# Stick-breaking attention: key blocks from last to first in three groups, and the order of the heads' steps on each engine

## The reference, cut to what matters

```python
q = rmsnorm(qkv[:, :, 0], q_norm)      # k likewise, v as it is
for blk in range(S // 128):            # queries q0 .. kend
    z = einsum("bhtd,bhsd->bhts", q[:, :, q0:kend], k[:, :, :kend]) * scale
    strict = key < query
    log_1mb = where(strict, log_sigmoid(-z), 0.0)
    between = cumsum(log_1mb, axis=3, reverse=True) - log_1mb
    att = where(strict, exp(log_sigmoid(z) + between), 0.0)
    out = einsum("bhts,bhsd->bhtd", att, v[:, :, :kend])
```

## Time and profile before

| | busy us | share of the span |
|---|---|---|
| TensorE (PE) | 3024.0 | 98% |
| VectorE (DVE) | 2709.6 | 87% |
| GpSimd (POOL) | 1680.2 | 54% |
| ScalarE (ACT) | 1495.0 | 48% |

### The profile page before, as it was taken

The page is one execution under the profiler, slowest core; times in us unless marked ns, Lnnn a source line. Parts: engine busy times, 40 slices in busy tenths (PEclk is TensorE's granted clock), DMA queues, the critical chain, the costliest instruction groups (busy, mean ns, idle before and its releaser), DMA issues.

```text
span 3098.5 us, 45070 instructions
## 1 busy us (share of the span) xinstructions
PE 3024.0 (98%) x15648; PEld 2701.9 (87%) x15648; DVE 2709.6 (87%) x4904; ACT 1495.0 (48%) x2668; POOL 1680.2 (54%) x989
## 2 busy tenths in 40 slices
PE   7999999999999999999999899999999999999999
PEld 6888899999999888888777678999999998888887
DVE  7987997999999889998687769989999999888887
ACT  4344335766665333343444643346666663333332
POOL 3434356888896555542245433467988986422221
PEclk9999999999999999999899899999999999999999
DMA  6633246999999999999335342357999999999996
GB/s 258 241 103 123 82 150 214 317 336 356 323 343 368 382 386 393 382 392 375 111 110 175 84 134 82 106 183 259 362 334 337 346 342 378 381 373 368 350 350 234
DMA packets 320605, 846.16 MB, mean 273 GB/s; under 512 B 28208, under 2 KB 149056, under 8 KB 320400
## 3 DMA queue, kind: packets, MB, share of 16 engines
q1 hardware_dynamic: 189952, 437.83, 41.0%
q0 software_dynamic: 74000, 268.81, 23.6%
q10 hardware_dynamic: 56448, 136.86, 11.7%
HBM read 735.91 MB, written 94.90 MB: 268 GB/s over the span
## 4 chain that ended last, share of the span: by engine, by line
PE 80%; DVE 11%; ACT 3%; issue 2%; POOL 2%; DMA 2%; SPq 0%; ACTq 0%; DVEq 0%; POOLq 0%
PE banks L1179 22%; PE gbank L1179 11%; PE banks L1159 9%; PE banks L1161 9%; PE banks L1160 9%; PE banks L1139 4%; PE banks L1141 4%; PE banks L1140 4%; DVE u_rows L2151 3%; PE gbank L1531 2%; POOL w_lo L593 1%; DVE hot L2128 1%; PE gbank L1485 1%; PE banks L1251 1%; POOL u_rows L610 1%
## 5 line engine op out<-in xcount | busy, mean ns | idle before, releaser
L593 POOL TENSOR_TENSOR w_lo<-raw,w_hi 128x1024 fp32r<-128x1024 f32 x351 | 868.7, 2476 | 567.6 <-ACT w_hi L685 563.7
L685 ACT ACTIVATE w_hi<-raw 128x1024 fp32r<-128x1024 f32 x613 | 646.8, 1055 | 603.6 <-PE banks L1179 350.5
L618 POOL DMA_INDIRECT v_rows<-v_dram,row_of x256 | 376.6, 1471 | 598.6 <-DVE fetched L2166 585.1
L1159 PE MATMUL banks<-h_hi,w_hi 128*128 128x384 f32 x2048 | 686.6, 335 | 2.7 <-POOL w_lo L593 2.7
L1160 PE MATMUL banks<-h_lo,w_hi 128*128 128x384 f32 x2048 | 684.7, 334 | 0.0
L1161 PE MATMUL banks<-h_hi,w_lo 128*128 128x384 f32 x2048 | 684.5, 334 | 0.0
L2151 DVE CUSTOM_DVE_ANT_0 u_rows<-u_rows,h_rows 128x1024 f32<-128x1024 f32 x256 | 449.8, 1765 | 5.3 <-DMA u_rows<-u_dram,row_of 5.2
L610 POOL DMA_INDIRECT u_rows<-u_dram,row_of x256 | 359.7, 1405 | 135.3 <-DVE z L2151 97.0
L1159 PEld LDWEIGHTS banks<-h_hi,w_hi 128*128 128x128 f32 x2048 | 384.7, 188 | 4.4 <-POOL w_lo L593 4.4
L1160 PEld LDWEIGHTS banks<-h_lo,w_hi 128*128 128x128 f32 x2048 | 384.5, 188 | 0.0
L1161 PEld LDWEIGHTS banks<-h_hi,w_lo 128*128 128x128 f32 x2048 | 384.4, 188 | 0.0
(11 more groups left out here) (377 smaller groups left out, 5079.2 us busy)
## 6 DMA issues: line engine op xcount, KB each, us to landing
raw<-stream_dram SPq DMA_DIRECT2D x613, 512.0 KB, 6.3
gel_dram<-gel ACTq DMA_DIRECT2D x248, 192.0 KB, 5.0
gin<-gel_dram SPq DMA_DIRECT2D x62, 768.0 KB, 10.5
g_dram<-stage ACTq DMA_DIRECT2D x56, 768.0 KB, 11.0
gates<-g_dram SPq DMA_DIRECT2D x64, 672.0 KB, 7.4
ada_w<-ada_dram ACTq DMA_DIRECT2D x34, 512.0 KB, 6.3
ada_out<-ada_dram ACTq DMA_DIRECT2D x18, 512.0 KB, 4.8
ada_first<-ada_dram SPq DMA_DIRECT2D x8, 1024.0 KB, 17.6
```

Of the source, the lines that this page charges most:

```text
L593: pool.tensor_tensor(w_lo[:, s, :], raw[:, s, :], w_hi[:, s, :].bitcast(F32), ALU.subtract).then_inc(split_lo, 1)
L618: pool.indirect_dma_start(v_rows[:, j % V_ROWS, :], None, (v0, v1)[layer], bass.IndirectOffsetOnAxis(ap=row_of[:, j:j + 1], axis=0)).then_ ...
L685: act.activation(w_hi[:, s, :], raw[:, s, :], ACT.Copy).then_inc(split_hi, 1)
L1159: pe.matmul(out, wh, h_hi[:, k, 0:DENSE_T], start=(k == 0), stop=False)
```

## The change

Three things change. First, the key blocks are kept and worked in the order 3, 2, 1, 0, in three groups: blocks 3 and 2 together (384 columns), block 1 (384), block 0 (512). ScalarE, VectorE and GpSimd do one instruction a group in place of one a block; the mask of blocks 3 and 2 is one product. Second, each wait of the products, of the casts and of the weights counts groups: the products of keys n start when the high part of their group is there, and `sp_hi` of h+1 may be rewritten group by group. Third, the order of the heads' steps is another on every engine: TensorE does the products of h, the logits of h+2, the weighted sum of h; ScalarE the Exp and Ln of h, the weights of h-1, the output copy of h-2; VectorE the sign passes of h, the output's low part of h-3, the max passes and low parts of h. GpSimd splits one side (q or k) after each head, where it split both after every second. Three constant tiles move to the place of a tile of layer 0. `att` stays one buffer.

```diff
@@ -166,7 +166,7 @@
 LOW_ROW = 32
 
 
-KEY_AT = [sum(SEQ - n * P for n in range(j)) for j in range(CH)]
+KEY_AT = [sum(SEQ - n * P for n in range(j + 1, CH)) for j in range(CH)]
 KEPT_KEYS = sum(SEQ - n * P for n in range(CH))
 STACKED = 6 * 16
 STACK_FROM = 21
@@ -175,6 +175,11 @@
 def from_key(j):
 
     return slice(KEY_AT[j], KEY_AT[j] + SEQ - j * P)
+
+
+GROUPS = 3
+GROUP_OF = (2, 1, 0, 0)
+GROUP_KEYS = (slice(0, from_key(2).stop), from_key(1), from_key(0))
 
 OUT_DOTS, V_DOTS, QKV_DOTS = 6, 18, 12
 V_COL = OUT_DOTS
...
@@ -437,13 +442,17 @@
 
 
         b = (bank, misc)[h % 2][min(j, 2)]
-        return b[:, 0:P] if j == 3 else b[:, n * P:]
+        return b[:, P:2 * P] if j == 3 else b[:, n * P:]
+
+    def zgroup(h, g):
+
+        b = (bank, misc)[h % 2][2 - g]
+        return b[:] if g == 2 else b[:, P:]
 
     def obank(h):
 
         return (bank, misc)[h % 2][3]
 
-    together = (1, 2, 4, 4)
 
     block = ctx.enter_context(nc.Block())
 
...
@@ -641,17 +650,21 @@
 
         lows(RING, DENSE0 + U_EARLY + LOW_AHEAD)
         peer(0)
-        def split_heads(m):
+        def split_side(m, n):
 
             pool.wait_ge(S("qk_done"), DC + m + 1)
             for half in range(2):
                 wait(pool, S(f"stacked{half}"), STACKED * (m - 1))
-            for n, x in enumerate((aq, ak)):
-                pool.tensor_copy(qk_hi[:, m % 2, n, :], x[:, m, :]).then_inc(S("qk_hi"), 1)
-            for n, (lo, x) in enumerate(((q_lo, aq), (k_lo, ak))):
-                pool.wait_ge(S("qk_hi"), 2 * m + n + 1)
-                pool.tensor_tensor(lo[:, m, :], x[:, m, :], qk_hi[:, m % 2, n, :].bitcast(F32), ALU.subtract
-                                   ).then_inc(S("qk_lo"), 1)
+            x, lo = ((aq, q_lo), (ak, k_lo))[n]
+            pool.tensor_copy(qk_hi[:, m % 2, n, :], x[:, m, :]).then_inc(S("qk_hi"), 1)
+            pool.wait_ge(S("qk_hi"), 2 * m + n + 1)
+            pool.tensor_tensor(lo[:, m, :], x[:, m, :], qk_hi[:, m % 2, n, :].bitcast(F32), ALU.subtract
+                               ).then_inc(S("qk_lo"), 1)
+
+        def split_heads(m):
+
+            for n in range(2):
+                split_side(m, n)
 
         lows(DENSE0 + 2 * NKEYS, QKV1 + 13)
         split_heads(0)
@@ -660,15 +673,15 @@
         lows(QKV1 + 17, OUT1 + LEAD)
         def stick_highs(h):
 
-            wait(pool, S("logw"), CH * h)
-            for j in range(CH):
-                pool.wait_ge(S("sp"), CH * h + j + 1)
-                pool.tensor_copy(sp_hi[:, from_key(j)], sp[:, h % 2, from_key(j)]).then_inc(S("sp_hi"), 1)
+            for g, own in enumerate(GROUP_KEYS):
+                wait(pool, S("logw"), GROUPS * (h - 1) + g + 1 if h else 0)
+                pool.wait_ge(S("sp"), GROUPS * h + g + 1)
+                pool.tensor_copy(sp_hi[:, own], sp[:, h % 2, own]).then_inc(S("sp_hi"), 1)
 
         for h in range(SB_HEADS):
             stick_highs(h)
-            if h % 2 == 0 and h // 2 + 2 < DC:
-                split_heads(h // 2 + 2)
+            if h // 2 + 2 < DC:
+                split_side(h // 2 + 2, h % 2)
         lows(OUT1 + LEAD, DENSE1 + U_EARLY + LOW_AHEAD)
         peer(1)
 
@@ -1086,18 +1099,19 @@
 
         def sticks(h):
 
-            for j in range(CH):
-                act.wait_ge(S("z_abs"), CH * h + j + 1)
-                zs = sp[:, h % 2, from_key(j)]
+            for g, own in enumerate(GROUP_KEYS):
+                act.wait_ge(S("z_abs"), GROUPS * h + g + 1)
+                zs = sp[:, h % 2, own]
                 act.activation(zs, zs, ACT.Exp, scale=-1.0).then_inc(S("z_exp"), 1)
-                act.wait_ge(S("z_exp"), CH * h + j + 1)
+                act.wait_ge(S("z_exp"), GROUPS * h + g + 1)
                 act.activation(zs, zs, ACT.Ln, bias=1.0).then_inc(S("z_ln"), 1)
 
         def weights(h):
-            for j in range(CH):
-                act.wait_ge(S("logw"), CH * h + together[j])
-                wait(act, S("att_out"), h)
-                act.activation(att[:, from_key(j)], zq(h, j, j), ACT.Exp).then_inc(S("att"), 1)
+
+            wait(act, S("att_out"), h)
+            for g, own in enumerate(GROUP_KEYS):
+                act.wait_ge(S("logw"), GROUPS * h + g + 1)
+                act.activation(att[:, own], zgroup(h, g), ACT.Exp).then_inc(S("att"), 1)
 
         def mixed(h):
             o = HD * (h % 2)
@@ -1105,13 +1119,14 @@
             act.activation(h_hi[o:o + HD, h // 2, :], obank(h)[o:o + HD, :], ACT.Copy
                            ).then_inc(S("o_hi"), 1)
 
-        sticks(0)
         for h in range(SB_HEADS):
-            if h + 1 < SB_HEADS:
-                sticks(h + 1)
-            if h:
-                mixed(h - 1)
-            weights(h)
+            sticks(h)
+            if h >= 1:
+                weights(h - 1)
+            if h >= 2:
+                mixed(h - 2)
+        weights(SB_HEADS - 1)
+        mixed(SB_HEADS - 2)
         mixed(SB_HEADS - 1)
         projected_out(1)
         peer(1)
@@ -1587,50 +1602,56 @@
 
             q, k_hi, k_lo_ = (stacks[h % 2][:, n, :] for n in range(3))
             pe.wait_ge(S(f"stacked{h % 2}"), STACKED * (h // 2 + 1))
-            for j in range(CH):
-                if 2 <= h and j < 3:
-                    pe.wait_ge(S("att"), CH * (h - 2) + together[j])
+            for j in (3, 2, 1, 0):
+                if h >= 2 and j != 2:
+                    pe.wait_ge(S("att"), GROUPS * (h - 2) + GROUP_OF[j] + 1)
                 for k in (k_hi, k_lo_):
-                    pe.matmul(zq(h, j, j), k[:, j * P:(j + 1) * P], q[:, j * P:], start=(j < 3 and k is k_hi),
+                    pe.matmul(zq(h, j, j), k[:, j * P:(j + 1) * P], q[:, j * P:], start=(j != 2 and k is k_hi),
                               stop=False, skip_group_check=True)
-                last = pe.matmul(zq(h, j, j)[:, 0:P], identb[:], masked[:], start=False, stop=True,
-                                 skip_group_check=True)
-                if j != 2:
-                    last.then_inc(S("z"), 2 if j == 3 else 1)
+                if j == 2:
+                    both = [P, 2, P]
+                    diag = zgroup(h, 0)[:, 0:2 * P].rearrange("p (j t) -> p j t", j=2)
+                    pe.matmul(diag, identb[:], masked[:].unsqueeze(1).to_broadcast(both), start=False, stop=True,
+                              skip_group_check=True).then_inc(S("z"), 1)
+                elif j < 2:
+                    pe.matmul(zq(h, j, j)[:, 0:P], identb[:], masked[:], start=False, stop=True,
+                              skip_group_check=True).then_inc(S("z"), 1)
 
         def log_weights(h):
 
-            pe.wait_ge(S("sp_hi"), CH * (h + 1))
-            pe.wait_ge(S("sp_lo"), CH * (h + 1))
-            for j in range(CH):
+            pe.wait_ge(S("sp"), GROUPS * (h + 1))
+            for n in (3, 2, 1, 0):
+                if n != 2:
+                    pe.wait_ge(S("sp_hi"), GROUPS * h + GROUP_OF[n] + 1)
                 for part_ in (sp_hi, sp_lo):
-                    last = pe.matmul(zq(h, j, j), negtri_r[:], part_[:, from_key(j)], start=False, stop=True,
+                    if n != 2 and part_ is sp_lo:
+                        pe.wait_ge(S("sp_lo"), GROUPS * h + GROUP_OF[n] + 1)
+                    last = pe.matmul(zq(h, n, n), negtri_r[:], part_[:, from_key(n)], start=False, stop=True,
                                      skip_group_check=True)
-                    for n in range(j + 1, CH):
+                    for j in range(n):
                         last = pe.matmul(zq(h, j, n), negones_r[:], part_[:, from_key(n)], start=False,
                                          stop=True, skip_group_check=True)
-                if j != 2:
-                    last.then_inc(S("logw"), 2 if j == 3 else 1)
+                if n != 3:
+                    last.then_inc(S("logw"), 1)
 
         def weighted(h):
             both = slice(P * (h // 2), P * (h // 2) + P)
             if h >= 2:
                 pe.wait_ge(S("o_hi"), h - 1)
                 pe.wait_ge(S("o_lo"), h - 1)
+            pe.wait_ge(S("att"), GROUPS * (h + 1))
             for j in range(CH):
-                pe.wait_ge(S("att"), CH * h + j + 1)
                 last = pe.matmul(obank(h)[:, j * P:], av[:, j, both], att[:, from_key(j)],
                                  start=(j == 0), stop=(j == CH - 1), skip_group_check=True)
             last.then_inc(S("att_out"), 1)
 
-        logits(0)
+        for h in range(2):
+            logits(h)
         for h in range(SB_HEADS):
-            if h + 1 < SB_HEADS:
-                logits(h + 1)
-            if h:
-                weighted(h - 1)
             log_weights(h)
-        weighted(SB_HEADS - 1)
+            if h + 2 < SB_HEADS:
+                logits(h + 2)
+            weighted(h)
         pe.wait_ge(S("o_lo"), SB_HEADS)
         for m in range(N_OUT - 2):
             h_tile(OUT1 + m)
@@ -2274,24 +2295,27 @@
         link(biased(2 * DC, OUT1_COL))
```

(51 more changed lines are left out.)

## The result

The changed kernel took 3077.56 us (median of 4 runs, 3076.86 to 3081.25) against 3099.84 for the kernel before (median of 4): the ratio is 0.9932, with a 95% interval of 0.9915 to 0.9949, so 22.3 us less where 21.0 were forecast. The profiled execution took 3076.86 us, 23.4 less than the profiled one before.

What follows compares the result with a forecast made beforehand. Layer 1's attention was taken as bound by a ring of waits between engines, no engine full. Fifteen heads of 7.1 us plus a 15.9 us last frame end it at 1799.8, 21.0 less: 3100.3 to 3079.3, range 3071 to 3092.

Steps and rivals of the forecast that it cites:

- The ring, and what opens it: Layer 1's attention: no engine full; removing TensorE's 2.31 us gap before logits keeps the clock up, saving 1.66 us a pair.
- VectorE's frame: One head's passes on VectorE in layer 1's attention: period 7.15 us for twelve heads, 6.85 for three, mean 7.1.
- TensorE: TensorE's work in one head: 6.6 us at the higher clock, under the period, with 0.5 us of slack.
- Merging: Three groups instead of four instructions a head: 0.47 us less on VectorE, 0.40 on ScalarE, about 0.1 on GpSimd.
- Rival (d): New head order does nothing, only merged instructions count: 7.5 us less, 3092.8; shares the chances of (a) and (b).
- The output's low part: VectorE's 0.69 us low-half output, moved three heads later, fills time in which VectorE would wait for ScalarE.
- Single buffers: One buffer of weights costs nothing; first and second groups of logs may slip about 0.3 us in VectorE's idle time.
- Tail: Two heads in flight lengthen the attention's last frame: 15.9 us, including 1.0 for a slow weighted sum.
- The sum: Frame 15 opens at 1783.9, stage ends at 1799.8 against 1820.78: 21.0 us less, forecast 3079.3, chance 0.70.
- (a): TensorE's clock lost in every second head: mean period 7.7 us, 11.5 less, 3088.8; 0.14 with the better half of Rival (d).
- (b): Small idle lowers TensorE's clock in every head: period 8.3 us, 2.5 less, 3097.8; 0.09 with Rival (d)'s worse half.
- (c): The products on TensorE lose the higher clock as well: period say 10.1 us, 25 more, 3125; chance 0.07.

Runs made afterwards that it cites:

- Weighted sum first: Changed kernel, but TensorE does the weighted sum of h ahead of the logits of h+2: 8.37 us a head, 3097.5 us.
- split later: Changed kernel, but GpSimd waits for all low parts of h before splitting a side: 6.61 us a head, 3068.7 us; again, 3074.5 us.
- both of these: Changed kernel with the edits of split later and first sign pass early together: 6.57 us a head, 3075.7 us.
- first sign pass early: Changed kernel, but VectorE does the first group's sign pass of h+1 ahead of the last subtraction of h: 6.57 us a head, 3067.9 us (one run).

## Why the prediction was right, point by point

**The ring, and what opens it.** Right. The prediction put the gain in the gap ahead of the logits and the lower clock behind it. The gap of 2.31 is 0.16 or nothing, and the 1.66 us a pair that the slow logits and weighted sums cost is gone. *Weighted sum first* shows that it is the place of the logits.

**VectorE's frame.** The mechanism was right, the size 0.33 us off: 7.15 predicted for the heads with a split, 6.82 measured. The mis-sized term is the step from recorded lengths to starts. I laid lengths end to end with gaps between them, but here a next line often starts about 0.08 before the recorded end. Two places of this are on the ring: ScalarE's six passes take 3.24 (1727.61 to 1730.85), not 3.44, so that its last Ln ends at 3.82 of the frame and not at 4.01, and the last max pass takes 0.60 to the next start, not 0.72. The three sign passes take 1.53 to the next start, not 1.79, but only the first of them is on the ring; the rest is idle time of VectorE (0.62 and 0.46 in turn, against 0.4). The kernel before shows it too: the first four sign passes take 1.76 in the earlier trace rows, where their four lengths make 1.9. The sum for the subtractions was right (2.37 to the next start against 2.35), its parts only roughly: the split was given 0.35 of it, and *split later*, which takes it away, saves 0.2 (2.11 and 2.20 to the next start).

**TensorE.** 6.6 predicted, 6.68 in the trace, 6.57 as the floor that *both of these* and *first sign pass early* reach. That it stays below the ring was right, with less to spare than given: 0.14 to 0.25 and not 0.5.

**Merging.** Predicted as 0.47 us a head of VectorE's work. Off the ring most of it is worth nothing: 0.13 in the new order. Rival (d) had it as 7.5 us of the whole with the order of before; there, groups and group-wise waits took 11.8 us, and with them the gap became short enough to keep the clock. The merging alone in the order of before was not run.

**The output's low part.** Right that it fills a wait; put on the ring it costs 1.05, of which 0.7 is its own.

**Single buffers.** Right in kind: group-wise waits keep the casts just in time. Their worth was not priced in the prediction; it is 0.45 us a head.

**Tail.** 15.9 predicted, 15.2 measured (1780.91 to 1796.14); the slow weighted sum in it did not come.

**The sum.** Fifteen frames 103.1 against 106.5, tail 15.2 against 15.9: a stage of 118.3 against 122.4. Against this, 1.4 us of the 103.1 is the hitch of the third head, foreseen nowhere, and 1.6 us was lost outside the stage, which the prediction took to be the same in both. The stage gained 25.0 us where 21.0 were forecast; that the whole came out at 22.3 less, so near, is in part luck.

**Rivals.** (a), (b) and (c) all needed a clock lost to small gaps. In mid-stage, gaps of up to 1.7 us in five kernels left it at 1.00. The Trainium skill (TensorE: Matmul & The Clock Gate, the section on psum-queue depth-cycling) reports of another kernel that micro-idles between groups made the clock oscillate; in mid-stage the traces of this case do not agree at such sizes, with 17.4 us of such waits in 11 places of *weighted sum first* at a granted clock of 1.00. In the stage's opening it is less clear: see the last section.

**What was said to show it.** Idle under 0.8, gaps under 0.6, clock over 0.97, the last low part near 1799: met, the last at 1796.1, but for the wait of ScalarE for the sign pass, said to stay near 39.0. It is 27.5.

## What to carry to other kernels

Where several engines pass tiles round, write one frame of each queue in order with starts and needs, and close the ring; then look at which step an in-order queue puts ahead of the one the next frame is waiting for. Take the spacing from start to start in the trace rather than from the recorded lengths. When one engine is relieved and the next floor is 0.25 us away, as here, further edits to the same ring buy only that, and fewer instructions count for little once they are off it.

## What the runs showed of the hardware

- VectorE and GpSimd slow each other in SBUF by an amount that depends on who was first. The same three subtractions took 2.03 to 2.33 us in heads 12, 14 and 15, without splits, 2.45 to 2.72 beside casts and splits, and 3.10 with GpSimd ahead of them, whose own cast and subtraction then took 0.61 and 1.46 in place of 0.93 and 2.06. That the order of arrival is the cause is read from two traces, not tested by itself.
- TensorE's clock: after gaps of 0.8 to 1.7 us in mid-stage it stayed at the higher level of 2.4 GHz (granted 1.00); after gaps of 2.31 us and 3.52 us it fell to the lower one of 1.2 GHz (granted 0.50), and came back within the next 6 us of work. The length of the gap does not decide alone: in the stage's opening, behind a wait for the second head's stack, the clock stayed at 1.00 after 1.62 us in the first profile of the changed kernel and fell after 1.68 us in the second (0.54 from 1682 to 1685 us). What else decides was not tested.
- Code that is the same up to the attention reaches it at 1673.7 to 1683.2 us. The stretch after takes 1275.9 to 1281.0 us. In the two kernels that were profiled twice, the opening moved by 0.7 and 4.7 us, the stretch after by 2.4 and 3.7, and the stage that was changed by 1.4 and 1.6.
